# Hybrid transformer block on one core: reciprocal norms spread through a row in memory instead of a product of ones with a diagonal array

## The reference, cut to what matters

```
def rmsnorm(x, g):
    y = xf * lax.rsqrt(jnp.mean(xf * xf, axis=-1, keepdims=True) + EPS)
    return y * g

u = rmsnorm(h, attn_norm_g);  proj = u @ w_in          # queries, keys, values of two attentions
h = h + concat(oA, oB) @ w_out
z = rmsnorm(h, mlp_norm_g) @ w_up
h = h + square(relu(z)) @ w_down
gate = sigmoid(rmsnorm(h, ple_norm_g) @ w_ple_gate)
h = h + gate * (p @ w_ple_proj)
return rmsnorm(h, final_norm_g)
```

## Time and profile before

| | |
|---|---|
| median of 3 runs | 1216.71 us (1216.58 to 1216.93) |
| profiled execution | 1215.57 us, of which the span from first to last instruction is 1213.7 |
| TensorE busy | 1191.8 us, 98% of the span; mean granted clock 0.996 |
| VectorE, ScalarE, GpSimd busy | 710.8, 518.6 and 600.2 us |
| transfers | 125.75 MB, 104 GB/s over the span |

### The profile page before, as it was taken

The page is one execution under the profiler, slowest core; times in us unless marked ns, Lnnn a source line. Parts: engine busy times, 40 slices in busy tenths (PEclk is TensorE's granted clock), DMA queues, the critical chain, the costliest instruction groups (busy, mean ns, idle before and its releaser), DMA issues.

```text
span 1213.7 us, 14773 instructions
## 1 busy us (share of the span) xinstructions
PE 1191.8 (98%) x5825; PEld 964.1 (79%) x5825; DVE 710.8 (59%) x927; ACT 518.6 (43%) x858; POOL 600.2 (49%) x284
## 2 busy tenths in 40 slices
PE   6999999999999999999999999999999999999997
PEld 5787787877677788888888888888888888888886
DVE  5245556566767457783937829478294692544233
ACT  6435445455655554423424243243342433442223
POOL 3323222232425567655565556655466555565542
PEclk8999999999999999999999999999999999999999
DMA  6811011123612333425234252342523423121203
GB/s 220 282 36 35 18 36 30 40 53 70 191 36 73 101 125 150 177 70 199 95 122 139 70 183 100 134 139 70 176 102 127 151 70 139 52 78 55 58 1 139
DMA packets 104123, 125.75 MB, mean 104 GB/s; under 512 B 21801, under 2 KB 87382, under 8 KB 98678
## 3 DMA queue, kind: packets, MB, share of 16 engines
q1 hardware_dynamic: 103814, 124.18, 31.2%
q10 hardware_dynamic: 240, 0.62, 0.1%
HBM read 111.14 MB, written 16.01 MB: 105 GB/s over the span
## 4 chain that ended last, share of the span: by engine, by line
PE 94%; DVE 3%; ACT 2%; DMA 1%; SPq 0%; issue 0%; DVEq 0%; ACTq 0%
PE ps L1811 51%; PE ps L1495 23%; PE ps L1471 8%; PE ps L1606 3%; PE ps L1629 3%; PE ps L1617 1%; PE ps L1693 1%; PE ps L1679 1%; PE ps L1666 1%; DMA x_raw<-in_x 1%; ACT e_a L1099 1%; PE ps L1538 1%; PE ps L1554 0%; PE ps L1509 0%; PE ps L1799 0%
## 5 line engine op out<-in xcount | busy, mean ns | idle before, releaser
L883 POOL TENSOR_TENSOR w_lo<-w_raw,w_hi 128x1024 fp32r<-128x1024 f32 x57 | 137.9, 2419 | 148.0 <-ACT w_hi L1008 146.9
L1811 PE MATMUL ps<-block_lo,w_hi 128*128 128x512 f32 x472 | 181.1, 389 | 0.0
L1495 PE MATMUL ps<-u_hi,w_hi 128*128 128x512 f32 x416 | 176.3, 424 | 3.8 <-DVE o_bt L2090 1.7
L752 POOL TENSOR_TENSOR w_lo<-w_raw,w_hi 128x1024 fp32r<-128x1024 f32 x38 | 96.1, 2529 | 163.9 <-ACT w_hi L1023 163.9
L1811 PE MATMUL ps<-up_hi,w_hi 128*128 128x512 f32 x448 | 174.9, 390 | 0.0
L1811 PE MATMUL ps<-up_hi,w_lo 128*128 128x512 f32 x448 | 174.3, 389 | 0.0
L1811 PE MATMUL ps<-up_lo,w_hi 128*128 128x512 f32 x448 | 174.3, 389 | 0.0
L1811 PE MATMUL ps<-block_hi,w_hi 128*128 128x512 f32 x440 | 172.0, 391 | 0.0
L1811 PE MATMUL ps<-block_hi,w_lo 128*128 128x512 f32 x440 | 171.3, 389 | 0.0
L1495 PE MATMUL ps<-u_hi,w_lo 128*128 128x512 f32 x416 | 163.4, 393 | 0.0
L1495 PE MATMUL ps<-u_lo,w_hi 128*128 128x512 f32 x416 | 162.8, 391 | 0.0
(11 more groups left out here) (224 smaller groups left out, 2091.8 us busy)
## 6 DMA issues: line engine op xcount, KB each, us to landing
up_lo<-lo_save SPq DMA_DIRECT2D x36, 1024.0 KB, 5.5
w_raw<-in_w_in SPq DMA_DIRECT2D x48, 256.0 KB
w_raw<-in_w_down SPq DMA_DIRECT2D x18, 512.0 KB
w_raw<-in_w_up SPq DMA_DIRECT2D x16, 512.0 KB
raw_x<-in_w_up SPq DMA_DIRECT2D x15, 512.0 KB
raw_x<-in_w_down SPq DMA_DIRECT2D x14, 512.0 KB
x_raw<-in_x SPq DMA_DIRECT2D x8, 512.0 KB, 7.3
h_save<-x_t SPq DMA_DIRECT2D x1, 4096.0 KB, 12.8
```

The source lines that it names most:

```text
L752: nc.gpsimd.tensor_tensor(w_lo[:, s * D:(s + 1) * D], w_raw[:, s * D:(s + 1) * D], w_hi[:, s * D:(s + 1) * D].bitcast(F32), ALU.subtract). ...
L883: nc.gpsimd.tensor_tensor(w_lo[:, s * D:(s + 1) * D], raw, w_hi[:, s * D:(s + 1) * D].bitcast(F32), ALU.subtract).then_inc(lo_done, 1)
L1495: mm = nc.tensor.matmul(bank(bank_), w, xx[:, x0], start=(first and n == 0), stop=(last and n == 2))
L1811: mm = nc.tensor.matmul(o, w, xx, start=(first and m == 0), stop=(last and m == 2), skip_group_check=onto)
```

## The change

The diagonal array, the product with ones and the copy out of PSUM go. In their place ScalarE issues two transfers: `send_rows` writes the 1024 numbers of `rs8` into a row of 1024 in memory (each of them 4 bytes, since partition q holds tokens q, 128+q, ...), and `read_rows` reads that row of 4 KB into all 128 partitions of `rstd`. VectorE waits for the second one (`rstd_in`) where it waited for ScalarE's copy. TensorE no longer waits for the row ahead of Q0. For norm 2 it writes banks 4 and 5 once with an ordinary product (`write_whole`) where the spread stood, since VectorE's sum in these banks is later added to by products that don't start them; VectorE waits for that too (`whole`). For norm 3 the second turning of `p` waits for the means and not for the row, and gate block 1 no longer waits for them.

```diff
+        rs_row = [nc.dram_tensor(f"rs_row{n}", [T], F32).ap() for n in range(3)]
...
-            def take_rstd(n, bank_):
-
-                act.wait_ge(rs_ps, n)
-                nc.scalar.copy(rstd[:, :], bank(bank_, 2)).then_inc(rstd_ok, 1)
+            def send_rows(n):
+                act.wait_ge(pow_ok, n)
+                act.dma_start(rs_row[n - 1].rearrange("(t q) -> q t", q=P), rs8[:, :], allow_slow_non_contiguous=True).then_inc(rs_out, 16)
+
+            def read_rows(n):
+                act.wait_ge(rs_out, 16 * n)
+                act.dma_start(rstd[:, :], rs_row[n - 1].partition_broadcast(P)).then_inc(rstd_in, 16)
...
+            send_rows(1)
             early_hi(2)
-            take_rstd(1, 6)
+            read_rows(1)
             early_hi(3)
...
                 copy_third(c)
+                if c == 0:
+                    send_rows(2)
                 sum_hi(up_product(c, 4), slot[1], s_dve, 2 * g + 2)
                 if c == 0:
-                    take_rstd(2, 4)
+                    read_rows(2)
...
-            take_rstd(3, 6)
+            send_rows(3)
+            read_rows(3)
...
-            half_block(1, 1, range(0, 4))
-            spread(1, 6)
-            half_block(1, 1, range(4, 8)).then_inc(blk_done, 1)
-
-            pe.wait_ge(rstd_ok, 1)
+            half_block(1, 1, range(DT)).then_inc(blk_done, 1)
...
+            def write_whole(b):
+                pe.wait_ge(mean_ok, 2)
+                w0, x0 = up_product(0, 3) % 2 * D, up_hi_at(UP[3])
+                for i in range(2):
+                    mm = nc.tensor.matmul(bank(b + i), w_hi[:, w0:w0 + P], up_hi[:, x0:x0 + HALF], start=True, stop=True)
+                mm.then_inc(whole, 1)
...
-                        spread(2, 4)
+                        write_whole(4)
...
-            pe.wait_ge(mean_ok, 3)
-            gate_block(1, hooks={3: lambda: spread(3, 6), 5: turn_second})
+            gate_block(1, hooks={5: turn_second})
...
-                diagonals(n)
-                dve.wait_ge(rstd_ok, n)
+                dve.wait_ge(rstd_in, 16 * n)
...
                     first_blocks()
-                    diagonals(2)
-                    dve.wait_ge(rstd_ok, 2)
+                    dve.wait_ge(rstd_in, 32)
+                    dve.wait_ge(whole, 1)
                 plus_third(c, d, 2)
```

More of the change, by code:

```diff
@@ L234, in build @@
         rstd = at("rstd", [P, T], F32, a_rstd)
-        diag = at("diag", [P, TT * P], F32, a_rstd)
         acc_mlp = at("acc_mlp", [P, T], F32, a_rstd)
@@ L339, in build @@
         mean_ok, pow_ok = sem("mean_ok"), sem("pow_ok")
-        diag_ok, rs_ps, rstd_ok = sem("diag_ok"), sem("rs_ps"), sem("rstd_ok")
+        rs_out, rstd_in = sem("rs_out"), sem("rstd_in")
+        whole = sem("whole")
         h_saved = sem("h_saved")
@@ L1503, in half_block @@
                 return mm
[L1505 to L1511, removed]
             def bank_for(name, half):
@@ L1948, in turn_second @@
             def turn_second():
-                pe.wait_ge(rstd_ok, 3)
+                pe.wait_ge(mean_ok, 3)
                 turn_ple(1)
@@ L2060, in mean_square @@
                 nc.vector.tensor_scalar(mean[:, :], sums_, 1.0 / D, EPS, ALU.mult, ALU.add).then_inc(mean_ok, 1)
[L2062 to L2067, removed]
             dve.wait_ge(x_ss, TT)
             mean_square(1, ssq[:, :])
-            diagonals(1)
-            dve.wait_ge(rstd_ok, 1)
+            dve.wait_ge(rstd_in, 16)
             for b, dst in enumerate((v_raw, k_b[0])):
```

## The result

The change makes the kernel slower: **1245.49 us** in the median of 4 runs (1244.69 to 1248.22) against 1216.64 of the kernel before beside it, a ratio of 1.0242 with a 95% interval of 1.0224 to 1.026. The forecast was 1215.8 and its range ended at 1222.5. The profiled execution took 1245.58 us.

The account below looks back on a forecast made before the run. TensorE was taken to bound the kernel, through its work and whether rows arrive on time. Norms 1, 2 and 3 gave -1.0 + 1.4 - 1.3 = -0.9 us, so 1216.7 became 1215.8 us; range 1213.0 to 1222.5 (8 in 10).

Parts of the forecast that it names:

- What bounds the kernel: Whole kernel: TensorE, busy 1191.8 of 1213.7 us; what counts is work leaving its list and rows arriving on time.
- the price of the write: Write of 4 KB in 1024 pieces: 4.3 us, between bounds 3.1 and 7.0; 5.5 at norm 1.
- The rival of small, slow pieces: Write at all norms takes 7 us or above: sum +5.2, 1221.9 us; chance 0.22.
- Its 8.8 us: Norm 2's write and read together: beyond this, norm 1's gain is spent and each further microsecond costs two.
- The fit from its section "Anatomy of one DMA": Both transfers: about 2.0 us plus bytes at 436 GB/s, so write 2.0, read 3.2, and everything hidden.
- The read: 512 KB into 128 partitions: 3.5 us where queues are nearly empty, 4.0 where SyncE has transfers, as at norm 2.
- That all partitions read one row: The read: all 128 partitions reading the same 4 KB, seen in no row, priced at nothing, upper end left open.
- Norm 1: Row at 54.2 us, behind `h_save`, V1 at 59.6; 0.7 of 1.7 us lost, so a gain of 1.0 us.
- The rival that `h_save` catches the transfers: Norm 1: write lands with `h_save` at 53, row at 57.5, V1 2.3 us later; 1219.1 us, chance 0.08.
- Norm 2: Row at 485.45 us; TensorE stands still 2.7 us and product 4 starts 1.4 us later than before.
- Norm 3: Row at 1103.75 us; `ple(0)` starts at 1106.25, 1.3 us earlier than before.
- The clock: Behind norm 2's 2.7 us stall the clock falls, costing 1.7 to 3.4 us: 1217.5 to 1219.2 us; chance 0.12.

Follow-up runs that it names:

- the first experiment: The changed kernel with the write in 128 pieces of 32 bytes, the row in another order so the output differs: 1215.43 us, ratio 0.9985.
- The probes: The kernel before plus extra small transfers whose data nobody uses, two runs: nine, 1227.92 us against 1216.88; eight at other spacings, 1218.04 against 1216.87.
- the turned row: The changed kernel, but TensorE turns the roots into 8 x 128, ScalarE copies them and writes 8 pieces of 512 bytes: 1219.27 us, ratio 1.0015.
- 32-byte pieces: The changed kernel with the write in 32-byte pieces and VectorE reading the row with a step of eight numbers, output correct: 1237.9 us, ratio 1.0171.
- a run tested that at norm 2 alone: The changed kernel with 62 matmuls instead of 2 in `write_whole`, so TensorE doesn't stand still at norm 2: 1246.01 us, ratio 1.0229.
- the best version: Changed kernel writing 8 turned pieces of 512 bytes, `h_save` sent behind norm 1's row, norm 2's wait behind `plus_third`: 1215.84 us, ratio 0.9989.

## Why the prediction was wrong

**What bounds the kernel** was right: TensorE's work and three deadlines. In the first experiment, where no row is late at norms 2 and 3, product 4 and `ple(0)` start 1.1 and 1.8 us earlier relative to the mean than before, close to the 1.3 and 1.7 that the removed work should give with everything on time.

**The step that failed is the price of the write**, the term 4.3 us with the bounds 3.1 and 7.0. It measured 10.5 and 11.3 at norms 2 and 3 (12.0 at norm 1, where I had 5.5). I built it from a fixed 1.4 us and the rate of 512-byte pieces, and took the 1024 pieces of 1 KB of `p` for the ceiling, since they move 256 times the bytes. Both rows show the cost of a piece that goes to a place of its own. The probes show that the count was priced about right (1024 pieces apart take 2.7 us) and that the length comes from the 4-byte neighbours, for which the trace of before had no row. I said that the write's length could make me wrong most, and then let a bound from rows of another kind close the range. The rival of small, slow pieces named the right term and that each microsecond of it counts twice, but put it at 7 us: chance 0.22 and 1221.9 us, 23.6 too low. Its 8.8 us are the point where the sum is zero; by its own terms the doubling begins at a write of 3.9 us, where norm 3's row starts to be late. The Trainium skill, "DMA: Bandwidth & Descriptors", section "Specifications", gives 512 bytes as the least for full rate, and reading and writing back below it. It pointed to the right side; the runs don't bear it out as the price of size, since pieces of 32 bytes land in 1.4 us and 4-byte pieces 32 bytes apart in 2.7. The fit from its section "Anatomy of one DMA", 2.0 us for the write, is given there for transfers that GpSimd issues; the prediction applied it to ScalarE's, and the write took over five times as long.

**The read** at norm 2, 4.0 us in the sum, took 8.0: the write had dammed up SyncE's transfers, and the read met them. With the fast write of the first experiment it took 4.2 at the same place. At norm 3, where little was behind, it took 4.0 for my 3.5. That all partitions read one row has no price that these times show, as assumed.

**Norm 1**, -1.0 in the sum, came out at +6.4. I had the row at 54.2, just behind `h_save` at 53.2; it came at 62.0, since the write landed at 50.8 and not at 44.1 and `h_save` took 21.0 us and not 12.8. From the row to V1 5.2 us passed, as worked out (5.4). The rival that `h_save` catches the transfers is half right: it slows the read (13.4 us even behind a fast write, at most 5.0 once `h_save` is sent later), and the slow write slows it. So this term had a second error of its own: with the fast write the row came at 55.3 and not at 54.2, and norm 1 gained nothing where I had 1.0.

**Norm 2**, +1.4, came out at +11.7: a stall of 12.87 in place of 2.7, the difference being 6.2 from the write and 4.0 from the read. That it had no cover was right. **Norm 3**, -1.3, came out at +6.1: 17.9 us from the root to `ple(0)` in place of 10.4, 7.0 of the difference from the write and 0.5 from the read. The three places are 25.2 us above the sum (24.3 in place of -0.9).

**The clock** was a rival of its own, with 1.7 to 3.4 us for a stall of 2.7. The runs show it unchanged behind 3.1 us (the turned row, norm 2), at 0.50 behind 3.4 (32-byte pieces, norm 1), and at 0.50 behind 5.3 and behind 7.7 to 12.9. With the stalls as they came it adds most of the last 5.7 us; a run tested that at norm 2 alone.

## What to carry to other kernels

When a transfer turns numbers from partitions into a row of memory, look at where its smallest pieces land, not at its bytes: 4 KB in neighbouring 4-byte pieces took 10 to 12 us and slowed the transfers beside it, and one small transpose on the way, with 512-byte pieces behind it, took the kernel from 2.4% over its old time to 0.15%. Price a kind of transfer for which the trace has no row with an open upper end, above all where its length counts once at each use. And moving work from the bounding engine to a chain of two transfers pays only if the chain is shorter than the cover: here the product of ones cost TensorE 4.7 us net, and the best version got 0.1% of 1216 us back.

## What the runs showed of the hardware beyond that

- The slow write is bad to overlap with other transfers: while it ran at norm 2, SyncE's moved 12 to 33 GB/s after one burst, where 400 followed. Probes that nobody needed cost the kernel 11 us in one placing and 1.2 in another.
- Writing 4-byte neighbours costs 10 us, reading the same 1024 pieces 2.1.
- 16 neighbours of 4 bytes took 1.5 us, 128 took 7.9, 256 took 9.1, 512 took 10.6 and 1024 took 10.7: more a step than a rate.
- VectorE's scaling of 1024 columns takes 1222 ns with a factor that lies side by side, and 2142 with one that steps by eight numbers.
